# Reordering the mixer's third and fourth projection: compression branch moved ahead, two reciprocal roots on GpSimd, masks and key rotation exchanged

## The reference

```python
(a_q, a_k, a_v, b_cq, b_ckv, b_kr, c_q,
 c_kc, c_vc, c_ks, c_vs, c_kw, c_vw, c_gf) = jnp.split(u @ w_in, splits, axis=-1)
qa = apply_rope(rms_norm(heads(a_q, A_HEADS), a_qk_g[0]), cos64, sin64)
ka = apply_rope(rms_norm(heads(a_k, A_KV_HEADS), a_qk_g[1]), cos64, sin64)
qc = rms_norm(heads(c_q, C_HEADS), c_qk_g[0])
qc_rot = apply_rope(qc, cos64, sin64)
k_cmp = rms_norm(compress_blocks(heads(c_kc, C_KV_HEADS), c_cmp_pe[0], c_cmp_w1[0], c_cmp_w2[0]), c_qk_g[1])
v_cmp = compress_blocks(heads(c_vc, C_KV_HEADS), c_cmp_pe[1], c_cmp_w1[1], c_cmp_w2[1])
k_slc = apply_rope(rms_norm(heads(c_ks, C_KV_HEADS), c_qk_g[2]), cos64, sin64)
k_win = apply_rope(rms_norm(heads(c_kw, C_KV_HEADS), c_qk_g[3]), cos64, sin64)
```

## Time and profile before

| what | value |
|---|---|
| time, median of 3 runs | 1119.61 us (1118.16 to 1119.70) |
| the profiled execution's own time | 1120.81 us |
| its span | 1119.0 us |
| TensorE busy | 1079.7 us, 96% |
| VectorE busy | 824.5 us, 74% |
| ScalarE busy | 500.2 us, 45% |
| GpSimd busy | 12.0 us, 1% |
| chain that ended last, by engine | PE 87%, DVE 7%, ACT 2%, DMA 2% |

### The profile page before, as it was taken

One profiled execution on the slowest core, in us unless ns is written; L12 is line 12 of the kernel. 1 busy time (PEld: TensorE's weight loads), 2 busy tenths in 40 slices (PEclk: granted clock), 3 DMA queues, 4 the chain that ended last, 5 costly groups with the idle time before them and its releaser, 6 DMA issues.

```text
span 1119.0 us, 13749 instructions
## 1 busy us (share of the span) xinstructions
PE 1079.7 (96%) x5217; PEld 834.0 (75%) x5221; DVE 824.5 (74%) x1458; ACT 500.2 (45%) x868; POOL 12.0 (1%) x30
## 2 busy tenths in 40 slices
PE   5999999999989999999999999999998999999998
PEld 1688888865766688888878888886567767888886
DVE  1766997876987885886687789887879787655644
ACT  2543442423577564343434433432265666443431
POOL 4000000000000000000000000000000000000000
PEclk9999999999989999999999999999998999999999
DMA  9899999455622179996439999964573213867532
GB/s 361 267 377 361 381 380 317 146 185 116 239 76 76 38 278 320 308 324 213 155 114 337 346 382 385 355 209 138 134 272 105 75 40 136 269 234 236 197 113 75
DMA packets 149365, 253.70 MB, mean 227 GB/s; under 512 B 9638, under 2 KB 119860, under 8 KB 141108
## 3 DMA queue, kind: packets, MB, share of 16 engines
q1 hardware_dynamic: 148596, 251.53, 65.4%
q10 hardware_dynamic: 704, 1.30, 0.3%
HBM read 251.76 MB, written 1.05 MB: 226 GB/s over the span
## 4 chain that ended last, share of the span: by engine, by line
PE 87%; DVE 7%; ACT 2%; DMA 2%; issue 1%; SPq 0%; DVEq 0%; ACTq 0%
PE ps L693 12%; PE ps L695 12%; PE ps L694 12%; PE ps L723 8%; PE ps L727 8%; PE ps L725 8%; PE ps L845 6%; DMA ada<-in_ada_w_dram 2%; PE ps L890 2%; PE ps L705 2%; PE ps L901 2%; PE ps L674 1%; PE ps L672 1%; PE ps L673 1%; PE ps L924 1%; PE ps L659 1%
## 5 line engine op out<-in xcount | busy, mean ns | idle before, releaser
L693 PE MATMUL ps<-wh,uh 128*128 128x512 f32 x576 | 227.3, 395 | 0.0
L695 PE MATMUL ps<-wlo,uh 128*128 128x512 f32 x576 | 224.6, 390 | 0.0
L694 PE MATMUL ps<-wh,ul 128*128 128x512 f32 x576 | 224.2, 389 | 0.0
L1645 DVE TENSOR_TENSOR wlo<-wide,wh 128x1024 fp32r<-128x1024 f32 x176 | 207.5, 1219 | 16.2 <-ACT wh L1183 14.5
L1183 ACT CAST wh<-wide 128x1024 fp32r<-128x1024 f32 x176 | 175.9, 1049 | 16.0 <-DMA wide<-in_ffn_w_in_dram 15.9
L1255 ACT ACTIVATE fs<-ps 128x512 f32<-128x512 f32 x40 | 24.0, 599 | 284.2 <-PE ps L695 275.1
L1800 DVE TENSOR_TENSOR fa<-fs,ps 128x512 f32<-128x512 f32 x40 | 27.5, 688 | 138.0 <-ACT fs L1255 137.4
L723 PE MATMUL ps<-th,fh 128*128 128x512 f32 x320 | 128.1, 400 | 0.0
L695 PEld LDWEIGHTS ps<-wlo,uh 128*128 128x128 f32 x576 | 108.1, 188 | 23.0
L727 PE MATMUL ps<-tlo,fh 128*128 128x512 f32 x320 | 124.9, 390 | 0.0
L725 PE MATMUL ps<-th,fl 128*128 128x512 f32 x320 | 124.6, 389 | 0.0
(11 more groups left out here) (363 smaller groups left out, 1534.6 us busy)
## 6 DMA issues: line engine op xcount, KB each, us to landing
wide<-in_ffn_w_in_dram SPq DMA_DIRECT2D x176, 512.0 KB, 6.6
ada<-in_ada_w_dram SPq DMA_DIRECT2D x60, 1024.0 KB, 7.2
tall<-in_ffn_w_out_dram SPq DMA_DIRECT2D x44, 1024.0 KB, 5.2
wide<-in_w_in_dram SPq DMA_DIRECT2D x14, 1024.0 KB, 7.7
tall<-in_w_out_dram SPq DMA_DIRECT2D x8, 1024.0 KB, 8.6
ada<-in_ada_w_dram SPq DMA_DIRECT2D x16, 512.0 KB, 6.0
wide<-in_c_cmp_w_dram SPq DMA_DIRECT2D x4, 1024.0 KB, 10.1
wide<-in_w_in_dram SPq DMA_DIRECT2D x4, 832.0 KB, 7.8
```

Of the source, the lines that this page charges most:

```text
L693: mm(o, uh[:, k, rows_], wh[:, hsl, :, k, :], start=(k == 0), stop=False, skip_group_check=True)
L694: mm(o, ul[:, k, rows_], wh[:, hsl, :, k, :], start=False, stop=False, skip_group_check=True)
L695: i = mm(o, uh[:, k, rows_], wlo[:, s, :, k, :], start=False, stop=(k == KD - 1), skip_group_check=True)
L1645: tt(wlo[:, n % 2, :, ks, :], raw, wh[:, (n + 1) % 2, :, ks, :].bitcast(F32), ALU.subtract)\
```

## The change

Four things, all in the mixer:

1. TensorE does `hid` ahead of the projection F_A, not behind it, and F_A is done in two parts: tile 0, then the transposes of `qb`, `kb` and `hidt`, then tile 1 with `w2` in its middle.
2. The fills of F_CQ and F_CK change slots: F_CQ now goes to the slot of F_CMPW and is loaded when `hid` is done; F_CK goes to the slot of F_A. ScalarE casts all four quarters of F_CQ right behind the silu, ahead of its copies of F_A, `qb` and `kb`. VectorE takes their rests and then the compressed key ahead of the norm and rotation of branch a. TensorE does the first quarter of F_CK ahead of the scores of unit 0.
3. Two roots (of F_CQ's heads and of the keys) are done by GpSimd, one `pow` instruction each on 16 and 8 elements in every partition; VectorE goes on and waits for the result where it needs it.
4. The masked compressed scores are taken at the end of loop step 1, where the rotation of the keys stood, and the rotation moves to step 2, behind `rescore(2)`. TensorE turns both halves of unit 1's probabilities ahead of the keys' transposes.

```diff
-F_LAT, F_CMPIN, F_A, F_CMPW, F_CQ, F_CK = range(6)
+F_LAT, F_CMPIN, F_A, F_CMPW, F_CK, F_CQ = range(6)
...
-                n += 1
+                n = WIDE_M + F_CQ
                 fill_wide(l, n, row_halves(n, 928),
+                          (aux_ready, aux_at(l, "hid")))
+                n = WIDE_M + F_CK
+                fill_wide(l, n, row_halves(n, 1696),
                           (proj, projected(l, F_A)))
-                n += 1
-                fill_wide(l, n, row_halves(n, 1696),
-                          (aux_ready, aux_at(l, "hid")))
...
-                project(l, F_A, 512, 0)
                 n = WIDE_M + F_CMPW
...
+                project(l, F_A, 512, 0, (0,))
                 for nm, src in (("qb", qb), ("kb", kb)):
...
+                project(l, F_A, 512, 0, (1,), compressed_kv)
                 pe.wait_ge(mod_red, rounds_at(l, 0, ROUNDS[0] + 1))
-                project_split(l, F_CQ, 2)
+                project_split(l, F_CQ, 0)
...
+                project_split(l, F_CK, 2, (0,))
                 pe.wait_ge(*aux_done("ka", l))
-                pe.wait_ge(pcopy, l * 10 + 6)
+                pe.wait_ge(pcopy, l * 10 + 8)
                 scores(l, 0)
-                project_split(l, F_CK, 2)
+                project_split(l, F_CK, 2, (1, 2, 3))
...
+            def root(l, which, n):
+                pool.wait_ge(root_in, 2 * l + which + 1)
+                tt(rst[:, 0:n], ssb[:, 0:n], half[:, :].broadcast_to([P, n]), ALU.pow).then_inc(root_out, 1)
...
-                for i in range(2):
-                    rescore(0, i)
                 copied(l, 3)
                 cq = v4(pq, C_H)
-                heads_rstd(cq, HD, v4(cq2[:, :, :], C_H))
+                mean_squares(cq, HD, v4(cq2[:, :, :], C_H))
+                for i in range(2):
+                    rescore(0, i)
+                rest_rows(F_CK, 3)
+                dve.wait_ge(root_out, 2 * l + 1)
...
                     if n == 2:
-                        compressed_scores()
+                        key_ropes(ck)
+                        compressed_shift()
...
                     if n == 1:
-                        key_ropes(ck)
+                        compressed_masks()
```

More of the change, by code:

```diff
@@ L176, in hybrid_kernel @@
         newt = sb("newt", [P, 32])
+        half = sb("half", [P, 1])
         ssb = sb("ssb", [P, 32])
@@ L436, in ffn_wide @@
                 elif f == 1:
-                    sp.wait_ge(proj, projected(l, (F_CQ, F_CK)[b]))
+                    sp.wait_ge(proj, projected(l, (F_CK, F_CQ)[b]))
                 elif l:
@@ L831, in aux_open, with project @@
                 return ps[:, 4 + g % 4, :]
-            def project(l, fill, width, banks):
+            def project(l, fill, width, banks, tiles=range(NT), interlude=None):
                 n = WIDE_M + fill
@@ L840, in project @@
                     pe.wait_ge(pcopy, l * 2 * len(CHUNKS) + 2 * (c if fill == F_CK else c - 1))
-                for t in range(NT):
+                for t in tiles:
                     for k in range(KD):
+                        if interlude and k == 4:
+                            interlude()
                         if fill == F_LAT:
@@ L849, in project, with project_split @@
                         turn_rows(l, 1, 1)
-            def project_split(l, fill, banks):
+            def project_split(l, fill, banks, quarters=range(4)):
                 n, c = WIDE_M + fill, CHUNKS.index(fill)
-                pe.wait_ge(pcopy, l * 2 * len(CHUNKS) + 2 * (c if fill == F_CK else c - 1))
+                pe.wait_ge(pcopy, l * 2 * len(CHUNKS) + 2 * (c - 1))
+                if fill == F_CQ:
+                    pe.wait_ge(pcopy, l * 2 * len(CHUNKS) + 2 * c)
                 pe.wait_ge(muh_ready, l + 1)
                 pe.wait_ge(mul_ready_, l + 1)
-                for q in range(4):
+                for q in quarters:
                     pe.wait_ge(mwh_ready, quarter_at(l, fill, q))
@@ L1260, in ffn, with copy_proj @@
                 last_block(l, f)
-            def copy_proj(l, chunk):
+            def copy_proj(l, chunk, tiles=range(NT)):
                 fill = CHUNKS[chunk]
-                bank = 2 if fill == F_CK else 2 * (chunk % 2)
-                for t in range(NT):
+                bank = {F_CQ: 0, F_CK: 2}.get(fill, 2 * (chunk % 2))
+                for t in tiles:
                     act.wait_ge(proj, l * 2 * len(CHUNKS) + (2 * chunk + t + 1))
@@ L1334, in mixer @@
                 A(hidr[64:64 + 2 * NCMP, :], ps[64:64 + 2 * NCMP, b, 0:P], ACT.Silu).then_inc(aux_act, 1)
+                for q in range(4):
+                    round_rows(F_CQ, q)
+                copy_proj(l, 2, (0,))
                 out_of(l, "qb0", qbT[:, 0:2, :], 96)
@@ L1343, in mixer @@
                                .unsqueeze(2).broadcast_to([P, 2, 4, NCMP])).then_inc(aux_act, 1)
-                for q in range(2):
-                    round_rows(F_CQ, q)
                 aux_wait(l, "w2")
@@ L1349, in mixer @@
                 nc.scalar.copy(vrep[:, :, :], ps[:, b, P:2 * P].rearrange("p (g n) -> p g n", g=2)).then_inc(aux_act, 1)
-                for q in range(2, 4):
-                    round_rows(F_CQ, q)
+                copy_proj(l, 2, (1,))
                 for q in range(3):
@@ L1470, in _ @@
             i.then_inc(tables, 1)
+            link(V.memset(half[:, :], -0.5))
+            def root(l, which, n):
+                pool.wait_ge(root_in, 2 * l + which + 1)
+                tt(rst[:, 0:n], ssb[:, 0:n], half[:, :].broadcast_to([P, n]), ALU.pow).then_inc(root_out, 1)
+            for l in range(DEPTH):
+                root(l, 0, NT * C_H)
+                root(l, 1, NT * 4)
         @block.vector
@@ L1916, in rest_rows @@
                        mwh[:, ks, :].bitcast(F32), ALU.subtract).then_inc(mwl_ready, 1)
-                copied(l, 2)
-                qk = v4(pa[:, :, 0:384], 6)
-                heads_rstd(qk, HD, v4(qk2[:, :, :], 6))
-                by_rstd(qk, qk)
-                for q in range(2):
-                    rest_rows(F_CQ, q)
-                link(rope(qk[:, :, 0:A_H, :], cs_of(T_AQ), [qa[:, :, :, :]]))
-                rope(qk[:, :, A_H:6, :], cs_of(T_AK), [kad[:, :, :, 0, :], kad[:, :, :, 1, :]]).then_inc(prep, 1)
-                dve.wait_ge(prep, prep_at(l, "qa"))
-                for q in range(2, 4):
+                for q in range(4):
                     rest_rows(F_CQ, q)
@@ L1937, in mixer @@
                 dve.wait_ge(prep, prep_at(l, "kc"))
+                copied(l, 2)
+                qk = v4(pa[:, :, 0:384], 6)
+                heads_rstd(qk, HD, v4(qk2[:, :, :], 6))
+                by_rstd(qk, qk)
+                link(rope(qk[:, :, 0:A_H, :], cs_of(T_AQ), [qa[:, :, :, :]]))
+                rope(qk[:, :, A_H:6, :], cs_of(T_AK), [kad[:, :, :, 0, :], kad[:, :, :, 1, :]]).then_inc(prep, 1)
+                dve.wait_ge(prep, prep_at(l, "qa"))
                 gates = gt[:, :, :].rearrange("p t (n g) -> p t n g", g=3)
@@ L1979, in mixer @@
                 dve.wait_ge(prep, prep_at(l, "cq"))
-                rest_rows(F_CK, 3)
                 normalise(0)
```

51 lines of the change are left out of this document (29 added, 22 removed).

## The result

The changed kernel takes 1124.9 us (median of 11 runs) against 1118.8 us for the kernel before, measured beside it: a ratio of 1.0055 (95% interval 1.0044 to 1.0066), or 6.1 us more. The profiled execution took 1123.97 us, with a span of 1122.2 us. One of the 11 executions took 1226.37 us at a granted clock of 0.849, in a slower state of the chip, and the ratio is taken without it. The profiled execution took only 3.2 us more than the profiled execution of before (1120.81 us). The gap between 6.1 and 3.2 comes from the two executions that were profiled: that of before took 2.0 us more than its median, that of the changed kernel 0.9 us less than its own.

The account below looks back on a forecast made before the run. TensorE, busy 96% of the span, was taken as the bound. Waits and second turn (+0.3 us a layer, +0.6 for both) plus a clock fall of 2.5 gave +3.1 us: 1122.7 us, range 1116.5 to 1126.5.

Parts of the forecast that it names:

- `hid` waits for its weights: TensorE ahead of `hid`, now before F_A: a new wait for weights, 0.8 us taken, bounds 0 and 1.1.
- `hidt` waits for `qb0`: TensorE between F_A's tiles: a new wait for ScalarE's copy behind four casts, 2.7 us taken, 2.2 to 3.1.
- The waits of 1.08 and 1.57 us: TensorE's old waits ahead of `w2` (copy of `hidt`) and at unit 0's scores (`kaT`): both removed in each layer.
- The sum at C: C is the end of projection F_CK; waits added and removed up to there: +0.8 us a layer, bounds -0.5 and +1.5.
- The clock: TensorE's granted clock falls behind the new wait at `hidt`: one fall, 2.5 us in all, bounds 0 and 6.8.
- Roots: Two `pow` per layer on GpSimd: under 1 us taken, bounds 0.1 and 4.4; hidden behind VectorE's work at 0.87 us.
- The keys: Keys' transposes behind F_CK: rotation ends at C+11.6, transposes now at C+11.5; TensorE waits some 2.4 us for `krd`.
- The gain of 0.5 us a layer from the second turn: Unit 1's second turn of probabilities, now done inside the wait ahead of the keys' transposes: -0.5 us a layer.
- if the clock at the keys stays up: Sign against the prediction: TensorE's clock not falling around the keys' transposes would make it wrong.
- The rival of a faster kernel: Clock spared at the keys, 1.4 us a layer: 1117.4 us, or 1115.0 if F_CQ's load lands sooner; chance 0.22.
- The late root: Rival: `pow` takes 4.4 us or more, the second root delays by 1.5 us a layer: 1123.2 us; chance 0.08.
- the blocked VectorE: Rival: VectorE's two-tile SBUF instructions wait while GpSimd works: +1.7 us, 1121.9; 3 in 100 of the late root's 8.

Follow-up runs that it names:

- Experiment 2: Changed kernel, with F_CQ waiting tile by tile for ScalarE's copies of F_A out of banks 0 and 1: 1123.23 us, ratio 1.0035 to the kernel before.
- experiment 4: Kernel before with only parts 3 and 4 of the change (roots on GpSimd; masks, rotation and second turn moved): 1118.53 us, ratio 0.9995.
- experiment 9: Changed kernel with two casts behind the copies, F_CQ's banks waited for tile by tile, and each root done twice: 1117.19 us, 0.9989 to the kernel before.

## Why the prediction was right, and where its sum was not

The forecast, slower through a wait ahead of `hidt` and a fall of the clock behind it, is what happened in direction and kind. In size it was half: +3.1 us forecast, 6.1 measured, because a wait of 1.21 us in each layer was left out. That 1124.9 us lies in the range of 1116.5 to 1126.5 owes something to luck: the range went that far up for falls of the clock, and the missing wait filled the room. Step by step:

- `hid` waits for its weights: 0.8 us taken as the mean of the layers, 0.88 and 0.73 measured (0.69 in the first layer of the second profile). Right.
- `hidt` waits for `qb0`: 2.7 us taken, 2.2 to 3.1 as bounds; 2.93 and 2.73 measured. Right, and for the reason given: casts, copy of the tile, half of `qb`.
- The waits of 1.08 and 1.57 us are gone. Right.
- The sum at C, +0.8 us a layer with bounds of -0.5 and +1.5, is wrong: +2.17 us in the second layer, where the clock stayed up, and 4.17 us in the first, where the waits (0.88 + 2.93 + 1.21 - 1.08 - 1.57 = 2.37) leave 1.8 for the clock. What is missing is one term. The prediction says that "None of this changes; only the waits do", but counts only the waits for data. It says nothing of the change of banks from `project_split(l, F_CQ, 2)` to `project_split(l, F_CQ, 0)`, a line that its own diff shows. F_A's tiles lie in banks 0 and 1. So F_CQ, which starts as soon as F_A ends, now has to wait until ScalarE has squared and copied the last tile out: 1.21 us in each layer. Experiment 2 takes that wait away. With it the sum is 0.8 + 1.2 = 2.0, which leaves 0.2 of the 2.17. The waits alone (2.37 us, and 0.73 + 2.73 + 1.21 - 1.08 - 1.57 = 2.02 in the second layer) are 4.4 of the 6.1 us.
- The clock: one fall of 2.5 us taken. In both profiles of the changed kernel it fell behind the wait in the first layer and not in the second, 0.57 of full speed over 4 us, which is 1.7 us. Right in kind and place, a little too large for one profile; for the mean over executions see the end of this section.
- Roots: "under 1 us" was taken for a `pow`; it is 2.93 us on 16 columns and 1.64 us on 8, within the bounds of 0.1 and 4.4. The nearest row was a poor guide. The cost of nothing was right in the changed kernel, since the cover held; on the kernel before (experiment 4) VectorE waited 0.63 us for the first root.
- The keys: C+11.6 forecast, C+11.65 measured in the changed kernel. The other profiles with one `pow` for each root agree (11.64 to 11.68, once 11.80) unless the clock fell early behind C or for long (12.10, 12.23 and 12.82). The gain of 0.5 us a layer from the second turn is not shown: parts 3 and 4 alone give a ratio of 0.9995, 0.3 us a layer, and its interval holds both 0 and 0.8. That TensorE would wait 2.4 us there was wrong in the profile (0.23), because the clock had fallen just ahead; where it had not, the waits were 0.66 and 1.84 us, 2.5 together.
- The sign "if the clock at the keys stays up" came true in both layers of the profile: the keys' transposes ran at the high clock, and the low stretch ended some 2 us ahead of them and was paid out of the wait. By its own words the prediction would have been wrong there. In that pair of profiles the rival's gain at the keys is real (1.8 and 1.9 us a layer from C to "next", where it took 1.4 for the clock and the sum 0.5 for the second turn); the medians show nothing of it. The likely reason is that the profiled execution of before was a slow one for its clock (0.992 over the span, 0.9965 in the mean), but no second profile of that kernel shows its keys. A sign that hangs on the clock of one execution was a poor test.

In the sum: forecast 0.6 + 2.5 = 3.1 us; measured 4.17 + 2.17 = 6.3 us up to C in the profile, against 6.1 in the medians. The rival of a faster kernel rested on a clock that stays up at the keys and a shorter wait at `hidt`; the second was not so. The late root did not occur.

Nor did the blocked VectorE. In the changed kernel `rescore(0)` inside the first root has nearly the durations that it has before (0.35 and 0.48 us, for 0.34 and 0.48), but it reads PSUM and so is no test. Experiment 4 is one: VectorE's subtraction of two tiles of SBUF began and ended inside the root and took its usual 1.22 us.

```profile
297.04 2.93 POOL L1477 TENSOR_TENSOR rst<-ssb,half 128x16 f32<-128x16 f32 x1 [275.48 <-DVE ssb L1522]
```

```profile
298.15 1.22 DVE L1932 TENSOR_TENSOR mwl<-wide,mwh 128x1024 fp32r<-128x1024 f32 x1
```

Of the two rules of the Trainium skill, "GPSIMD Engine Reference", "Instruction dispatch", gives about 6 us for the first call of a freshly loaded kernel. No such start is seen here: the first `pow` took 2.93 us and the one of the second layer 2.90, and each began at most 0.15 us behind the instruction that it waited for. But GpSimd had done TENSOR_TENSOR instructions before, in the kernel's setup, so these traces may hold no such first call. By "SBUF — State Buffer", "SBUF: two separate sides", of the Trainium skill the first to take the shared port pair keeps it for the whole instruction, against a VectorE operation with two SBUF inputs too. That does not agree with the rows of experiment 4, where the subtraction began 1.1 us behind `pow` and was not held up; its second layer has the same (838.20 us inside a `pow` from 837.02 to 839.91), and so has the second layer of experiment 9, where the second `pow` began at 841.08, 0.05 us ahead of the subtraction, and both had their usual lengths (2.89 and 1.24 us). The other way round, in the first layer of experiment 9 the second `pow` began 0.06 us after that subtraction and took 3.92 us instead of 2.9. Whether VectorE held it up there stays open.

Also open is how much of the 6.1 us the clock makes over many executions. The mean granted clock over the span is 0.9965 in 69 executions of the kernel before and 0.9953 in 15 of the changed one. If TensorE were busy in all of the additional low time, the difference of 0.0012 times 1119 us would cost 1.3 us, by the scatter of the executions 0.6 to 2.1 us.

## What to carry to other kernels

When an operation is moved, look at the bank that it writes as well as at what it reads: a projection that now follows the last user of its bank directly pays for that user's copy, here 1.2 us each time, and waiting for each tile's bank by itself takes it back. A copy that frees a bank for TensorE goes ahead of casts that nobody needs yet: the place of two casts on an engine that is 45% busy was worth about as much as the whole change lost. And before a fall of the clock is priced, ask whether TensorE waits at the end of the stretch: where it does, a fall that costs less than that wait can be paid out of it, if it does not slow the work that the other engine is waiting for.
